# Stick-breaking attention on one Trainium2 core: one-minus rows and part of the products on POOL

## The reference, cut to what matters

```
z = jnp.einsum('bqhd,bkhd->bhqk', q, k) * (SB_HEAD_DIM ** -0.5) + bias
mask = k_pos[None, :] < q_pos[:, None]
log_keep = jnp.where(mask, jax.nn.log_sigmoid(-z), 0.0)
log_after = lax.cumsum(log_keep, axis=3, reverse=True) - log_keep
a = jnp.where(mask, jnp.exp(jax.nn.log_sigmoid(z) + log_after), 0.0)
return jnp.einsum('bhqk,bkhd->bqhd', a, v)
```

## Time and profile before

| what | us |
|---|---|
| median of 3 runs (3248.36 to 3249.91) | 3248.76 |
| the profiled execution | 3256.13 |
| its span, first to last instruction | 3254.6 |
| the stage changed, from 1717.8 to 2025 in the span | 307 |
| of it PE busy, 1729 to 2025 | 240.88 |
| DVE, ACT, POOL busy there | 226.71, 199.09, 13.79 |

### The profile page before, as it was taken

The page is one execution under the profiler, slowest core; times in us unless marked ns, Lnnn a source line. Parts: engine busy times, 40 slices in busy tenths (PEclk is TensorE's granted clock), DMA queues, the critical chain, the costliest instruction groups (busy, mean ns, idle before and its releaser), DMA issues.

```text
span 3254.6 us, 52029 instructions
## 1 busy us (share of the span) xinstructions
PE 3009.7 (92%) x20232; PEld 2669.0 (82%) x20232; DVE 1758.9 (54%) x2649; ACT 1077.6 (33%) x1794; POOL 92.8 (3%) x163
## 2 busy tenths in 40 slices
PE   6996799999999999899966887999999999999997
PEld 6994699999999999799944444556899999999996
DVE  4016225666666666610035777555335666666666
ACT  5223223222222222522245666454133222222221
POOL 0010000000000000000001000000000000000000
PEclk8998899999999999899978889999999999999998
DMA  4122211111111111122242111999311111111101
GB/s 135 48 96 78 63 39 33 39 53 44 39 39 39 58 39 39 56 75 80 80 135 62 32 34 37 357 390 390 120 33 40 39 45 51 39 39 39 58 26 67
DMA packets 188140, 260.61 MB, mean 80 GB/s; under 512 B 9560, under 2 KB 138222, under 8 KB 188044
## 3 DMA queue, kind: packets, MB, share of 16 engines
q1 hardware_dynamic: 170752, 197.23, 17.6%
q0 software_dynamic: 16512, 61.71, 6.0%
q10 hardware_dynamic: 780, 0.34, 0.0%
HBM read 238.24 MB, written 27.68 MB: 82 GB/s over the span
## 4 chain that ended last, share of the span: by engine, by line
PE 80%; ACT 6%; DVE 5%; DMA 4%; issue 2%; SPq 2%; ACTq 0%; POOL 0%; DVEq 0%; POOLq 0%
PE ps L320 23%; PE ps L321 23%; PE ps L322 22%; DMA pv_tail<-in_cache_sb_v_dram 2%; PE ps L994 2%; PE ps L429 2%; ACT brk_w L1041 1%; ACT left_w L1046 1%; DVE x L1966 1%; PE ps L979 1%; PE ps L1217 1%; PE ps L964 1%; PE ps L1256 1%; PE ps L1234 1%; ACT prob L1585 1%
## 5 line engine op out<-in xcount | busy, mean ns | idle before, releaser
L1966 DVE TENSOR_TENSOR x<-x,ps 128x512 f32<-128x512 f32 (+1 forms) x792 | 538.9, 687 | 305.7 <-PE ps L322 304.8
L320 PE MATMUL ps<-act_hi,w_hi 128*128 128x370 f32 x2112 | 702.3, 333 | 1.4 <-DVE act_lo L464 1.4
L321 PE MATMUL ps<-act_lo,w_hi 128*128 128x370 f32 x2112 | 701.4, 332 | 0.0
L322 PE MATMUL ps<-act_hi,w_lo 128*128 128x370 f32 x2112 | 699.6, 331 | 0.0
L320 PE MATMUL ps<-w_hi,act_hi 128*128 128x256 f32 (+1 forms) x1800 | 507.2, 282 | 3.4 <-DVE w_lo L316 2.0
L321 PE MATMUL ps<-w_lo,act_hi 128*128 128x256 f32 (+1 forms) x1800 | 506.6, 281 | 0.0
L322 PE MATMUL ps<-w_hi,act_lo 128*128 128x256 f32 (+1 forms) x1800 | 505.0, 281 | 0.0
L320 PEld LDWEIGHTS ps<-act_hi,w_hi 128*128 128x128 f32 x2112 | 398.7, 189 | 5.7 <-DVE act_lo L464 1.7
L321 PEld LDWEIGHTS ps<-act_lo,w_hi 128*128 128x128 f32 x2112 | 398.5, 189 | 2.0
L322 PEld LDWEIGHTS ps<-act_hi,w_lo 128*128 128x128 f32 x2112 | 397.9, 188 | 0.0
L316 DVE TENSOR_TENSOR w_lo<-w_raw,w_hi 128x2048 fp32r<-128x2048 f32 x73 | 167.3, 2292 | 357.2 <-ACT w_hi L312 357.2
(11 more groups left out here) (288 smaller groups left out, 3645.7 us busy)
## 6 DMA issues: line engine op xcount, KB each, us to landing
w_raw<-in_w_up_dram SPq DMA_DIRECT2D x88, 512.0 KB, 4.9
pk_w<-in_cache_sb_k_dram SPq DMA_DIRECT2D x64, 384.0 KB, 5.3
pv_w<-in_cache_sb_v_dram SPq DMA_DIRECT2D x64, 384.0 KB, 5.3
pk_tail<-in_cache_sb_k_dram SPq DMA_DIRECT2D x64, 384.0 KB, 5.5
pv_tail<-in_cache_sb_v_dram SPq DMA_DIRECT2D x64, 384.0 KB, 5.4
d_raw<-in_w_down_dram POOLq DMA_DIRECT2D x44, 512.0 KB, 3.8
projected<-stage POOLq DMA_DIRECT2D x13, 1024.0 KB, 5.2
w_raw<-in_w_in_b_dram SPq DMA_DIRECT2D x20, 512.0 KB, 4.3
```

The costliest lines, as they stand in the source:

```text
L320: pe.matmul(out, ahi, bhi, start=first, stop=False, **kw)
L321: pe.matmul(out, ahi, blo, start=False, stop=False, **kw)
L322: return pe.matmul(out, alo, bhi, start=False, stop=last, **kw)
L1966: dve.tensor_tensor(xs, xs, ps[0:ROWS[t], DN_BANK[(2 * t + c) % 4], :], ALU.add).then_inc(dn_ev, 1)
```

## The change

Four things are changed in the stage.

1. ACT no longer writes `left_w`, and DVE no longer writes `left_n`. POOL computes 1 - s with a `tensor_scalar` for all steps and both heads, 96 instructions in place of ACT's 96 (in chunks) and DVE's 48.
2. For wide steps the product of head 1 is done by POOL (`second`), 24 instructions. DVE keeps the product of head 0, and all of the narrow steps. PE's `turn(s, 0)` of a wide step waits for POOL's semaphore `bp_m` too.
3. `left_w` has two buffers instead of one. To make room, `sb_raw` moves into the memory of `w_raw`, which is idle in this stage; the first load of sample keys, which used that place, moves behind the last pair's `prep`.
4. The loads of q, k, v go through SP's queue instead of POOL's. Those of pair 0 are issued within `sp_ms`, after the first load of memory values; POOL's constants are made after the prompt's memory attention; PE starts `prep` of pair 0 once the sample memory attention's last output is ready (`ms_ok`), and ACT needs no `nbias12`.

The core of the diff:

```diff
-        left_w = r("left_w", [P, 2, SEQ + 1])
+        left_w = r("left_w", [P, 2, 2, SEQ + 1])
+        sb_raw = sb_at("sb_raw", [P, 2, NPT, P], w_hi_at + 4 * half)
+        def a_after(s, hh):
+            return 2 * s + hh + 1 - (s + 1 if wide(s) and hh else s) // 2
+        def sp_bp(sp):
...
+            def first():
+                sp.wait_ge(w_ok, out0[1] + 1)
+                sp.wait_ge(w_used, out0[1])
+                raw(0)
+                values(0)
         def pool_bp(pool):
-            pool.wait_ge(ms_lo, 4)
+            pool.wait_ge(mq_lo, 2 + 16)
...
+            pool.wait_ge(ms_lo, 4)
+            def second(s):
+                if wide(s):
+                    w = (step(s)[1] + 1) * P
+                    left, end = left_edge(s)
+                    row = breaks_of(s)[:, 1, 0:w]
+                    pool.wait_ge(bp_left, 2 * s + 2)
+                    pool.tensor_tensor(row, row, left[:, 1, end - w + 1:end + 1], ALU.mult).then_inc(bp_m, 1)
+                    pool.wait_ge(bp_m, s // 2 + 1)
+            for s in range(NSTEP):
+                w = (step(s)[1] + 1) * P
+                left, end = left_edge(s)
+                for hh in range(2):
+                    pool.wait_ge(bp_sig, sig_after(chunks(s)[-1][0], hh))
+                    ago = 4 if wide(s) else 2
+                    if s >= ago and not (hh and wide(s)):
+                        pool.wait_ge(bp_a, a_after(s - ago, hh))
+                    pool.tensor_scalar(left[:, hh, end - w:end], breaks_of(s)[:, hh, 0:w], -1.0, 1.0, ALU.mult,
+                                       ALU.add).then_inc(bp_keep, 1)
+                if s >= 2:
+                    second(s - 2)
+            second(NSTEP - 1)
         def pe_bp(pe):
-            pe.wait_ge(ms_lo, 4)
-            pe.wait_ge(masked, BP_MASKED)
+            pe.wait_ge(ms_ok, 4)
...
                 if f == 0:
-                    pe.wait_ge(bp_a, 2 * s + 2)
+                    pe.wait_ge(bp_a, a_after(s, 1))
+                    if wide(s):
+                        pe.wait_ge(bp_m, s // 2 + 1)
         def act_bp(act):
-                        if wide(s):
-                            if s >= 2:
-                                act.wait_ge(bp_a, 2 * (s - 2) + hh + 1)
-                            act.activation(left[:, hh, at + c0:at + c0 + w], z, ACT.Sigmoid, bias=nbias12[:, h:h + 1],
-                                           scale=-1.0).then_inc(bp_sig, 1)
         def dve_bp(dve):
-                    dve.wait_ge(bp_sig, sig_after(chunks(s)[-1][0], hh))
-                    if not wide(s):
-                        dve.tensor_scalar(c, row, -1.0, 1.0, ALU.mult, ALU.add).then_inc(bp_keep, 1)
-                        dve.wait_ge(bp_keep, s + hh + 1)
+                    dve.wait_ge(bp_keep, 2 * s + hh + 1)
...
-                    dve.wait_ge(bp_left, 2 * s + hh + 1)
-                    dve.tensor_tensor(row, row, left[:, hh, end - w + 1:end + 1], ALU.mult).then_inc(bp_a, 1)
-                    dve.wait_ge(bp_a, 2 * s + hh + 1)
+                    if not (hh and wide(s)):
+                        dve.wait_ge(bp_left, 2 * s + hh + 1)
+                        dve.tensor_tensor(row, row, left[:, hh, end - w + 1:end + 1], ALU.mult).then_inc(bp_a, 1)
+                        dve.wait_ge(bp_a, a_after(s, hh))
```

More of the change, by code:

```diff
@@ L160, in build @@
         mid = r.at
-        sb_raw = r("sb_raw", [P, 2, NPT, P])
         sb_qk0 = r("sb_qk0", [P, 2, SEQ])
@@ L255, in build @@
             sem("bp_" + n) for n in ("ld", "z", "sig", "keep", "left", "a", "t", "at", "av", "hi", "lo", "set", "one"))
-        bp_v = [sem(f"bp_v{h}") for h in range(2)]
+        bp_v, bp_m = [sem(f"bp_v{h}") for h in range(2)], sem("bp_m")
         bs_in, bs_set, bs_qt, bs_q, bs_tr, bs_qb, bs_kn, bs_ka, bs_kd, bs_z, bs_sig, bs_msk, bs_edge, bs_scan, \
@@ L853, in sig_after @@
         def sig_after(n, hh):
[L855 to L860, removed]
+            return 2 * n + hh + 1
         def blocks(s, f):
@@ L891, in build, with raw, values, rest @@
         sb_v = sb_at("sb_v", [P, 2, NPT, P], w_hi_at + (2 + idle_half) * half)
+        sb_raw = sb_at("sb_raw", [P, 2, NPT, P], w_hi_at + 4 * half)
         def breaks_of(s):
             return (brk_w if wide(s) else brk_n)[:, s // 2 % 2, :, :]
+        def a_after(s, hh):
+            return 2 * s + hh + 1 - (s + 1 if wide(s) and hh else s) // 2
         def left_edge(s):
-            return (left_w, SEQ) if wide(s) else (left_n, 512)
+            return (left_w[:, s // 2 % 2], SEQ) if wide(s) else (left_n[:, 0], 512)
+        def sp_bp(sp):
+            def raw(i):
+                for n in range(2):
+                    sp.dma_start(sb_raw[:, n, :, :], proj[0:SEQ, n * MIX + i * P:n * MIX + (i + 1) * P]
+                                 .rearrange("(t p) f -> p t f", p=P)).then_inc(bp_ld, 16)
+            def values(i):
+                sp.dma_start(sb_v[:, i % 2, :, :], proj[0:SEQ, 2 * MIX + i * P:2 * MIX + (i + 1) * P]
+                             .rearrange("(t p) f -> p t f", p=P)).then_inc(bp_v[i % 2], 16)
+            def first():
[3 more added lines that the diff above has]
+                values(0)
+            def rest():
+                for i in range(1, NPAIR):
+                    sp.wait_ge(bp_t, prep_no(i - 1, 3) + 1)
+                    raw(i)
+                    if i >= 2:
+                        sp.wait_ge(bp_av, av_after((i - 1) * NPT - 1))
+                    values(i)
+            return first, rest
         def pool_sb_out(pool):
@@ L1000, in pe_bp @@
                 prep(0, m)
+            pe.wait_ge(masked, BP_MASKED)
             scores(0)
@@ L1060, in act_bp @@
                 prep(0, m)
-            act.wait_ge(bp_one, 4)
+            act.wait_ge(bp_set, 16)
             breaks(0)
@@ L1076, in dve_bp @@
             dve.wait_ge(ms_lo, 4)
-            dve.memset(left_w[:, :, SEQ:SEQ + 1], 1.0).then_inc(bp_one, 1)
-            dve.memset(left_n[:, :, 512:513], 1.0).then_inc(bp_one, 1)
+            dve.memset(left_w[:, :, :, SEQ:SEQ + 1], 1.0).then_inc(bp_one, 1)
+            dve.memset(left_n[:, :, :, 512:513], 1.0).then_inc(bp_one, 1)
             dve.memset(zero1[:, :], 0.0).then_inc(bp_one, 1)
-            dve.wait_ge(bp_set, 16)
-            dve.tensor_scalar(nbias12[:, :], bias12[:, :], -1.0, None, ALU.mult).then_inc(bp_one, 1)
-            dve.wait_ge(bp_one, 4)
+            dve.wait_ge(bp_one, 3)
             dve.wait_ge(masked, BP_MASKED)
@@ L1151, in sp_bs @@
             sp.wait_ge(bs_set, 16)
-            sp.wait_ge(w_ok, out0[1] + 1)
-            sp.wait_ge(w_used, out0[1])
             def pages(b, g):
@@ L1185, in batch @@
                         new_values(b + 1)
-            keys(0, 0, pages(0, 0))
             page = [pages(0, g) for g in (0, 1, 2, 3)]
             sp.wait_ge(bp_t, prep_no(NPAIR - 1, 3) + 1)
+            keys(0, 0, page[0])
+            sp.wait_ge(bp_z, chunks((NPAIR - 1) * NPT - 1)[-1][0] + 1)
             sp.dma_start(qkn_raw[:, :, :], proj[SEQ:NTOK, 0:2 * MIX].rearrange("t (n f) -> t n f", n=2)).then_inc(bs_in, 16)
@@ L1657, in pe_mq, with sp_ms @@
             pe.wait_ge(mq_lo, 2 + 8 * (l + 1))
-        def sp_ms(sp, l):
+        def sp_ms(sp, l, then):
             def load(dst, name, gr):
@@ L1673, in sp_ms @@
             load(mvc[0], "cache_mem_v", 0)
+            if then:
+                then()
             sp.wait_ge(mq_nm, 9 * l + 9)
@@ L2072, in _ @@
                 load_cols(sp, out0[l], A["w_out"][l], 0)
-                sp_ms(sp, l)
+                pairs_first, pairs_rest = sp_bp(sp)
+                sp_ms(sp, l, pairs_first if l else None)
                 if l:
+                    pairs_rest()
                     sp_bs(sp)
```

20 lines of the change are left out of this document (1 added, 19 removed).

## The result

| | median, us | runs | profiled span, us | stage, us |
|---|---|---|---|---|
| before | 3249.34 (3248.36 to 3257.12) | 4 | 3254.6 | 307.6 |
| changed | 3365.78 (3361.81 to 3367.77) | 4 | 3365.8 | 425.4 |

The change makes the kernel slower: ratio 1.0358, 95% interval 1.0334 to 1.0382. "Stage" is measured here and in all that follows from DVE's last `act_lo` of 128x64 (the end of the sample memory attention) to the start of the last `act_lo` of 128x256. This makes it comparable, since executions come to it some microseconds earlier or later after identical code: here it begins at 1717.54 before and at 1712.01 after. It is 117.8 us longer and starts 5.5 us earlier, and the spans differ by 111.2: the whole loss lies in this stage.

What follows compares the result with a forecast made beforehand. The prediction took PE, waiting for ACT's copies of fills in wide steps, as the bound. It summed -41.1 + 110.6 + 1 + 14 - 8 = +76 us, giving 3325 us on the median, range 3285 to 3392.

Steps and rivals of the forecast that it cites:

- the main case: Whole kernel: +76 us to 3325 us, with a PE hole of 4 to 5.5 us per wide iteration; chance 0.52.
- ACT's waits gone: PE's waits for ACT's copies of fills in wide steps vanish: 23 times 1.79 us, -41.1 us.
- Sigmoid and POOL's start: Start of PE's hole: 0.90 us from scores to head 0's sigmoid, plus 0.28 us for POOL to react.
- Two one-minus rows: POOL's two rows within PE's hole, priced from its affine selects: 1.87 us for mean widths of 832 columns.
- The product: POOL's head 1 product within PE's hole, at twice the affine select's rate per column: 1.71 us for 832 columns.
- The holes in all: PE idle after the scores of wide iterations until POOL's product: 23 times 4.81 us, +110.6 us.
- The clock: PE's granted clock in the stage falls from 0.89 to 0.84 because of longer holes: +14 us.
- The head: Start of the stage: earlier loads on SP let PE's transposes of q start sooner, -8 us.
- the port rival: DVE's scan gets in ahead of POOL's product and lengthens PE's hole: +43 us, in all +119, 3368 us; chance 0.20.
- signs of being wrong: In the profile after: stage under 300 us, DVE scans stretched or beside idle POOL instructions, or PE waits under 2 us.
- the relief of ACT deciding: Head 1's product is ready when PE needs it, waits for ACT's copies go: 3195 us; chance 0.05.
- The cheap-POOL rival: POOL's product runs at the affine select's rate and the clock holds: +44 us, 3293 us; chance 0.20.

Runs made afterwards that it cites:

- the fill experiment: Changed kernel, but POOL writes a constant over the row in place of head 1's wide-step product: 3288.69 us in one run.
- the first experiment: Changed kernel, but POOL does the product of step s - 1, not s - 2, after the one-minus rows of step s: 3219.15 us, 0.9897 of before.

## Why the prediction was right, and where it was short

The direction, the cause and its place were right, and 3365.78 lies in the range of 3285 to 3392. The size of the main case was not: +76 us was forecast, and the stage became 117.8 longer. Point by point:

- **ACT's waits gone** (-41.1): 46.3 us became 4.5, -41.8. Right.
- **Sigmoid and POOL's start** (1.18 us): from the end of the scores at 1867.67 to POOL's row at 1868.48 it is 0.81. A little too dear.
- **Two one-minus rows** (1.87 on average, 2.0 for 896 columns): 2.12 at 1868.48. The affine select of the earlier trace rows was a good stand-in. POOL's load by columns was summed wrongly, though: by the prediction's own rates its rows and products make some 108 us, not 75. It did not enter the sum.
- **The product** (1.71 us): this is the term that failed. By the fill experiment it is worth 3.48 us, by the groups 3.20. Undisturbed it takes 2.16 us for 1024 columns and 1.54 for 640, against 2.07 and 1.35 by the prediction's formula, some 1.85 for the 1.71; so its own rate was nearly right, and the rest, 1.4 to 1.6 us, is the wait for DVE's scan. The Trainium skill's figure, page GPSIMD Engine Reference, section Performance versus the Vector engine (4497 ns for 2048 columns), halves to an estimate of 2.25 us for 1024, which agrees with the 2.16. For 832 columns it gives 1.83 us and 2.7 us more in all, where the prediction wrote 1.9 and 5.
- **The holes in all** (+110.6): 146.6 us, 36 more.
- **The clock** (+14 at 0.84): PE's busy time rose by 27.7 us at 0.75. The memory attention was a poor stand-in: PE's busy share is alike (62% there, 272.65 / 426 = 64% here), the granted clock is not. The conversion erred the other way: busy time times clock held constant, as the prediction did it, would make +45 us at 0.75, and 27.7 were measured. Behind such a hole four transposes take 1.09 us (1874.36) instead of 0.65 to 0.66.
- **The head** (-8): PE's transposes of q begin 7.92 us after the sample attention before and 0.48 us ahead of that point after the change, -8.4 us. Right in the profile; alone it is worth 5 to 6.5 us of the whole kernel by the timed runs, with a wide interval.
- **Small waits of PE** (not counted): some 7 us that are gone, those for `brk_w` of DVE and for rows of ACT.

The sum in the stage: -41.8 + 146.6 + 27.7 - 8.4 - 7 = 117.1, measured 117.8. It closes by its nature, since waits and busy time of PE make up the stage; it tells how large each part was, not why.

The likeliest case was given 3325 us; what came true is **the port rival** (3368 us, 0.20). Its mechanism is shown by the pairs of rows above, by the scan that keeps its 0.69 us beside the fill, and by POOL's product falling from 3436 to 2289 ns for the same form where it stands elsewhere in the order. Scans stretched beside POOL were also among the prediction's own signs of being wrong. Its sum was +43 us by 23 scans of 1.89; the holes measured 36 more than the main case. That its 3368 us are so near the 3365.78 is in part luck: its holes were 7 us too long, its clock term 14 us too small, and the 7 us of small waits were not in it. The prediction named the condition ("the scan gets in ahead of POOL's product"), and that scan and products read two inputs in SBUF, but gave it only 0.20, when no row of the kernel before showed the two engines together. A missing row is no evidence against a mechanism.

The other rivals: the relief of ACT deciding (3195 us) needed, as the prediction said, "another order of the work, which the code does not have". The experiments supplied it: 3219.15 with the product one step earlier, 3208.33 with it on DVE. They stay above 3195. In the first PE still waits 38.9 us ahead of wide steps; in the second 28.5 us for DVE, which nearly fills the stage. The prediction did not see this, since it costed DVE by its load of before with the hole beside it. The cheap-POOL rival falls with the measured 2.16 us and the clock of 0.75.

One thing follows for the experiments' own expectations: those by the port theory for the better order were too high (3240 to 3265 for the 3219.15, 3225 to 3245 for the 3208.33, which even lies where it was expected if the engines ran together). Contention lengthens instructions everywhere (a narrow product of 558 ns took 1624), but this only costs time where someone waits for that instruction; on DVE's slack it is free, ahead of PE's transpose it is 1.4 to 1.6 us each time.

## What to carry to other kernels

Before a bound engine waits for work on a helper engine, read what stands ahead of that work in the helper's own order, and whether any of it needs what the bound engine issued last: here one step's distance in a loop was worth 147 us, with the same instructions on both sides. Price work that is given to POOL beside a busy DVE with the DVE instruction it will meet, some 1.5 us on top of 1.85 in this kernel, not with its time alone. And when the first bound is lifted, cost the next one with what it now has to do: the freed ACT brought 27 us of stage, and then DVE was the bound, with 238 of 269 us, 26 of them contention.

## What the runs showed of the hardware

- DVE's scan with a second input in SBUF, even one that is a single broadcast column of zeros, and its products exclude POOL instructions that read SBUF, for the whole instruction, in either order of arrival: 896 columns 2.67 for 2.03 us, 256 columns 2.37 for 0.69, a product of 896 columns 2.71 for 1.09. A POOL fill is not excluded: 0.69 us for a scan of 256 columns beside it. A DVE instruction with one input in PSUM and one in SBUF is not held up either (0.42 us at 1748.77 of the first experiment), but DVE's one-minus row, with its one input in SBUF, is (547 ns on average for 291).
- POOL: a one-minus row of 1024 columns 1.05 us, a product of 1024 columns 2.16 us and one of 640 columns 1.54 undisturbed; its recorded duration includes the wait for the port, up to 3.7 us.
- A wait of PE for a semaphore of POOL is put down to "issue" in the profile; a large total under this name is a reason to look at the timeline.
- The granted clock, over each version's whole stage, went with the holes: 0.75 with 23 of 6.37 us, 0.85 with 22 of 3.68, 0.90 with 14 of 2.8 and 0.91 with 7 of 3.9, against 0.87 before with 29 of 1.6 and one of 8.2.
